# Three expert weight chunks loaded inside the last RWKV head pair, and token-row stores put behind four chunk loads

## The reference, cut to what matters

```python
for i in range(DEPTH):                       # DEPTH = 2
    h = rms_norm(x, norm_mix_g[i])
    mix = rwkv7_time_mix(h, ...) if i % 2 == 0 else mla_mix(h, ...)
    x = x + mix
    x = x + expert_choice_ffn(rms_norm(x, norm_ffn_g[i]), moe_router[i],
                              moe_w_gate[i], moe_w_up[i], moe_w_down[i])

def expert_choice_ffn(h, w_router, w_gate, w_up, w_down):
    aff = softmax(h @ w_router)                       # over 16 experts
    gates, idx = top_k(swapaxes(aff, 1, 2), 64)       # 64 tokens for each expert
    xe = h[b_idx, idx]
    hid = silu(xe @ w_gate) * (xe @ w_up)
    return zeros_like(h).at[b_idx, idx].add((hid @ w_down) * gates)
```

## Time and profile before

| what | value |
|---|---|
| timed runs, median (lowest to highest) | 1900.12 us (1898.45 to 1905.87) |
| profiled execution, own time | 1901.98 us |
| its span | 1900.2 us |
| TensorE busy in the span | 1772.0 us (93%) |
| VectorE, ScalarE, GpSimd busy | 819.0, 559.6, 153.1 us |
| bytes moved, mean | 459.69 MB, 242 GB/s |
| last RWKV pair, from its first to its last product | 529.6 to about 591.8 us |
| first product with an expert weight, layer 0 | 666.76 us |
| last product of layer 0's experts | about 1110 us |

### The profile page before, as it was taken

The page is one execution under the profiler, slowest core; times in us unless marked ns, Lnnn a source line. Parts: engine busy times, 40 slices in busy tenths (PEclk is TensorE's granted clock), DMA queues, the critical chain, the costliest instruction groups (busy, mean ns, idle before and its releaser), DMA issues.

```text
span 1900.2 us, 40296 instructions
## 1 busy us (share of the span) xinstructions
PE 1772.0 (93%) x17576; PEld 898.3 (47%) x17576; DVE 819.0 (43%) x1562; ACT 559.6 (29%) x1161; POOL 153.1 (8%) x230
## 2 busy tenths in 40 slices
PE   7999999999999599999988998999996999999998
PEld 4456666666555333333333355666543333333333
DVE  7867777776653412222211234777414222112212
ACT  3456555655542111111110123555320111101110
POOL 2101110111011100000000011111120000000000
PEclk9999999999999799999999998999997999999999
DMA  4101101110314999999999942000276999999998
GB/s 130 37 19 45 38 24 35 45 38 24 110 69 150 366 377 427 428 427 427 427 428 426 417 165 112 24 24 25 98 304 249 428 427 428 427 427 428 427 428 343
DMA packets 92184, 459.69 MB, mean 242 GB/s; under 512 B 16997, under 2 KB 50154, under 8 KB 68202
## 3 DMA queue, kind: packets, MB, share of 16 engines
q1 hardware_dynamic: 89994, 449.78, 58.5%
q0 software_dynamic: 2016, 7.34, 1.0%
HBM read 449.23 MB, written 7.86 MB: 241 GB/s over the span
## 4 chain that ended last, share of the span: by engine, by line
PE 73%; DMA 10%; issue 7%; DVE 3%; ACT 2%; SPq 2%; DVEq 1%; POOL 1%; POOLq 1%; another core or an unknown queue 1%; ACTq 0%; PEldq 0%
PE banks L1780 26%; PE banks L549 9%; DMA arena<-in_moe_w_down 7%; PE banks L1802 5%; PE banks L854 4%; PE banks L1433 4%; DMA arena<-in_moe_w_up 3%; PE banks L2355 3%; PE banks L2220 2%; PE banks L2380 1%; PE banks L2368 1%; PE banks L834 1%; PE banks L566 1%; SPq L1957 1%; PE banks L1748 1%
## 5 line engine op out<-in xcount | busy, mean ns | idle before, releaser
L1780 PE MATMUL banks<-arena 128*64 128x512 f32 x2944 | 657.4, 601 | 32.1 <-DMA arena<-in_moe_w_down 20.2
L1780 PEld LDWEIGHTS banks<-arena 128*64 128x64 f32 x2944 | 209.7, 138 | 442.7 <-issue 411.3
L1945 DVE TENSOR_TENSOR arena<-arena,banks 128x512 f32<-128x512 f32 x128 | 88.1, 688 | 285.1 <-PE banks L1802 285.1
L549 PE MATMUL banks<-arena 128*128 128x512 f32 x384 | 192.1, 618 | 0.0
L1885 ACT ACTIVATE arena<-banks 128x512 f32<-128x512 f32 x32 | 34.1, 1066 | 394.1 <-PE banks L1780 394.1
L1929 DVE SCALAR_TENSOR_TENSOR arena<-arena,banks 128x512 f32<-128x512 f32 x32 | 34.1, 1064 | 217.7 <-ACT arena L1885 217.7
L1802 PE MATMUL banks<-arena 128*128 128x512 f32 x256 | 114.7, 598 | 1.5 <-DVE arena L1942 1.5
L854 PEld LDWEIGHTS banks<-arena 64*64 64x64 f32 x5120 | 83.7, 134 | 62.9 <-issue 51.4
L1932 DVE SCALAR_TENSOR_TENSOR arena<-arena,small,banks 128x512 f32<-128x512 f32 x32 | 35.6, 1112 | 174.6 <-PE banks L1780 174.6
L854 PE MATMUL banks<-arena 64*64 64x64 f32 x5120 | 95.0, 221 | 2.6 <-issue 0.9
L549 PEld LDWEIGHTS banks<-arena 128*128 128x128 f32 x384 | 64.8, 189 | 51.5 <-issue 43.1
(11 more groups left out here) (307 smaller groups left out, 2217.7 us busy)
## 6 DMA issues: line engine op xcount, KB each, us to landing
arena<-in_moe_w_gate SPq DMA_DIRECT2D x64, 2048.0 KB, 32.5
arena<-in_moe_w_up SPq DMA_DIRECT2D x64, 2048.0 KB, 35.1
arena<-in_moe_w_down SPq DMA_DIRECT2D x54, 2048.0 KB, 36.2
arena<-in_moe_w_down SPq DMA_DIRECT2D x24, 512.0 KB, 11.6
arena<-in_moe_w_down SPq DMA_DIRECT2D x8, 1024.0 KB, 26.1
arena<-in_x SPq DMA_DIRECT2D x8, 512.0 KB, 7.5
arena<-in_rw_wr SPq DMA_DIRECT2D x8, 512.0 KB, 4.3
arena<-in_rw_wk SPq DMA_DIRECT2D x8, 512.0 KB, 4.2
```

What stands on the lines that cost most here:

```text
L549: last = nc.tensor.matmul(b[:, :], w_sl[:, n, k, :], xmix[n][:, k, :], start=(k == 0), stop=(k == ND - 1))
L1780: last = nc.tensor.matmul(b[z * CAP:(z + 1) * CAP, :], st[:, k, :], ring[g % RING][:, k, z * 512:(z + 1) * 512], start=(c % 2 == 0 and k = ...
L1945: nc.vector.tensor_tensor(xs, xs, b[:, :], ALU.add).then_inc(free[xj[("add", i, j)][0]], 1)
```

## The change

Placement. The tiles of the RWKV pairs are given new addresses. Eight prepared inputs (`rT, kT, kkn, kraw, cs, cx, e_neg, in_chunk`), `tw`, `ta`, the even parity of `AR` and `y_out` now fill the first three slots, `RING0` to `RING0 + 3 * CHUNK`. Tiles that the last pair, u = 7, still uses (`Bt`, `Kt`, the odd parity of `AR`, `rk_cols`, the block matrices) stay below `RING0`; `vT`, `ysq`, `bonus` go behind the third slot. No computing instruction is added, removed or reordered: the rows of TensorE, VectorE, ScalarE and GpSimd, with their waits, are the same in both kernels.

SP's program. In the last pair, before anything else of that pair, SP waits until the operands of pair 7 are complete, and then three times for a level of the inversion, `("U", 0, 1, 7)`, `("U", 2, 1, 7)` and `("U", 4, 1, 7)`, issuing chunk 0, 1 and 2 behind them. In layer 0 `load_experts` then starts with chunks 3, 8 and 10 alone, stores token tiles 0 and 1, loads 4, 5, 6 and 7, and stores tiles 2 and 3 behind chunk 7. Layer 1 keeps its order.

```diff
-        in_chunk = body(S)
         head_ones = body(P)
-
-        rT, kT, vT, kkn, kraw, cs, cx, rk_cols, e_neg = (body(S) for _ in range(9))
-        tw, ta = [body(S) for _ in range(2)], [body(S) for _ in range(2)]
+        rk_cols = body(S)
         Bt = [body(S) for _ in range(2)]
         Kt = [body(S) for _ in range(2)]
-        AR = [[body(2, NCH, CH) for _ in range(2)] for _ in range(2)]
+        AR_last = [body(2, NCH, CH) for _ in range(2)]
...
-        ysq = body(S)
+        PREPARED = 3
+        prepared = place(RING0)
+        in_chunk = prepared(S)
+        rT, kT, kkn, kraw, cs, cx, e_neg = (prepared(S) for _ in range(7))
+        tw, ta = [prepared(S) for _ in range(2)], [prepared(S) for _ in range(2)]
+        AR = [[prepared(2, NCH, CH) for _ in range(2)], AR_last]
+        y_out = [prepared(S) for _ in range(2)]
+        assert prepared.at[0] <= RING0 + PREPARED * CHUNK and NPAIR % 2 == 0
+
+        body = place(RING0 + PREPARED * CHUNK)
+        vT, ysq = body(S), body(S)
         bonus = [body(S) for _ in range(2)]
-        y_out = [body(S) for _ in range(2)]
...
-            for g in (0, 1, 2, 3, KEPT + 1, KEPT + 3) if layer == 0 else (0, 1, 2, 3, 4, KEPT + 1, KEPT + 3):
+            for g in (3, KEPT + 1, KEPT + 3) if layer == 0 else (0, 1, 2, 3, 4, KEPT + 1, KEPT + 3):
                 load_chunk(sp, layer, g)
...
-            for t in range(NT - 1):
+            for t in range(2 if layer == 0 else 3):
                 store_tokens(t)
             job_full(sp, ojs[layer], ("out", NT - 1, 1))
             for g in (4, 5, 6) if layer == 0 else (5, 6):
                 load_chunk(sp, layer, g)
             sp.wait_ge(hT_read[layer], 1)
             load_chunk(sp, layer, KEPT)
-            store_tokens(NT - 1)
+            for t in range(2 if layer == 0 else 3, NT):
+                store_tokens(t)
             sp.wait_ge(routed[layer], 1)
             load_chunk(sp, layer, KEPT + 2)
...
             for u in range(NPAIR):
+                if u == NPAIR - 1:
+                    sp.wait_ge(operands_ready, 2 * (NPAIR - 1))
+                    for g in range(PREPARED):
+                        job_full(sp, rj, ("U", 2 * g, 1, u))
+                        load_chunk(sp, 0, g)
                 if 0 < u < NPAIR - 1:
```

More of the change, by code:

```diff
@@ L157, in trunk @@
         eye = body(CH)
-        in_chunk = body(S)
         head_ones = body(P)
-        rT, kT, vT, kkn, kraw, cs, cx, rk_cols, e_neg = (body(S) for _ in range(9))
-        tw, ta = [body(S) for _ in range(2)], [body(S) for _ in range(2)]
+        rk_cols = body(S)
         Bt = [body(S) for _ in range(2)]
         Kt = [body(S) for _ in range(2)]
-        AR = [[body(2, NCH, CH) for _ in range(2)] for _ in range(2)]
+        AR_last = [body(2, NCH, CH) for _ in range(2)]
         blocks_at = body.at[0]
         body(ND * S)
+        assert body.at[0] <= RING0
         over = place(blocks_at)
```

## The result

The changed kernel took 1905.81 us (median of 20 runs, 1901.84 to 1908.62), the kernel before 1901.74 us (20 runs, 1897.84 to 1906.49). The ratio is 1.0020 with a 95% interval of 1.0012 to 1.0028, a loss of 2.3 to 5.3 us. It is measurable over 20 runs, but under the 0.5% at which one measurement of this kernel tells a change.

What follows compares the result with a forecast made beforehand. The prediction took layer 0 as bound by TensorE's start with the experts plus a fixed-length weight stream. Its terms, 0 + 0 + 0 + 3 + 0 = +3 us, gave 1903 us beside 1900.12, range 1895 to 1911.

Steps and rivals of the forecast that it cites:

- The bound: Layer 0's experts: the time TensorE begins with them, plus a weight stream of fixed length behind it.
- The rival by which the stream gains 14.7 us: Layer 0's experts: weights bound from the first chunk on, so 14.7 us leave the stage, 1885.4 us; chance 0.06.
- The early chunks' head start, 0: Layer 0's stream: loading chunks 0 to 2 in the last pair only lengthens DMA gaps; gain 0.
- The stores, 0: Stores of tiles 2 and 3, queued behind four chunks, stay hidden by 15 us of cover; cost 0.
- the addresses, 0: New tile addresses: no duration depends on the address; cost 0, bounds -1 to +1 us.
- Starved TensorE, +3: Last pair: early chunk loads delay TensorE's instruction fetch; cost 3 us, bounds 0 to 14 us.
- the step that I took from pair 6: Pair 6's idle beside the 4.2 MB projection load, which cost 5.2 us, taken as guide for the last pair's loads.
- What would show it: Changed profile's expected signs: issues near 545.4, 560.5, 571.4 us; idle of 0.5 to 2 us behind second and third chunks.
- my bound of 6: Last pair: the prediction is wrong if TensorE's "issue" idle grows by over 6 us.

Runs made afterwards that it cites:

- e9: Kernel before with chunks 8 and 10 loaded behind chunk 9, after the routing, instead of at 602 us; ratio 1.0027.
- e2: Changed kernel with only chunks 0 and 1 early, chunk 2 back at the head of the expert loads; ratio 1.0007 to the kernel before.
- e10: Kernel before with the projection load in four, new addresses, new store order and chunks 0 and 1 early; ratio 0.9999.
- e7: Kernel before with its 4 MB output projection load cut into four pieces spread through pair 6; 1897.69 us, ratio 0.9983.
- e1: Changed kernel without the early loads and with the old store order, so the new addresses alone; 1900.68 us, ratio 0.9994 to the kernel before.
- e5: Kernel before with the changed kernel's order of stores alone; ratio 1.0012.
- e11: Changed kernel with the old order of stores, all three chunks still early; ratio 1.0028 to the kernel before.
- e4: Changed kernel with 32 extra products in pair 0's bonus job, shifting TensorE's later code; ratio 1.0114 to the kernel before.
- e6: Changed kernel with chunk 2 alone early, chunks 0 and 1 back at the head of the expert loads; ratio 1.0020 to the kernel before.
- e3: Changed kernel with all three chunks issued in one burst behind the inversion's last level; ratio 1.0019 to the kernel before.

## Why the prediction was right

**The bound.** Right. Chunk 12 follows TensorE's use of chunk 1, 11.79 us behind the first expert product in all fourteen traces, however early the first eleven chunks came. The rival by which the stream gains 14.7 us failed at the point named, full slots and dry windows. What I did not size was how much slack that is; e9 puts it near 5.6 us.

**The early chunks' head start, 0.** Right: no gain in the changed kernel, in e2 against before or in e10 against e7.

**The stores, 0, and the addresses, 0.** e1 bears out the second within 0.14%. For the first e5 and e11 leave 0.2% either way.

**Starved TensorE, +3.** The mechanism was right, and the step that I took from pair 6; e4 and the times of the packets show it. That the size came out near is in part luck. I chose 3 out of bounds of 0 to 14, by bytes and with a discount for the late onset; the timed loss is 4.07 us between medians, and the stretch from L999, where chunk 2's cost lies, is 2.3 us longer in the profiled execution (3.8 in e6, 4.1 in e3 and e11). The split was less good. I gave 0.5, 1 and 1.5 us to chunks 0, 1 and 2; measured were 0, 0.26 and 1.99 us of idle, so chunk 2 was under-sized and the others over-sized. What makes the difference is where a block border falls, which I had no count for; e4, with 128 records of shift, gives 1.74 us to chunk 1 and 0.38 to chunk 2. I also left the clock behind the idle out of the 3 us. It was granted at 0.58 and 0.57 in e6 and e11, which cost 1.7 and 1.6 us beside the idle, and at 1.00 in the profiled execution of the changed kernel. That such spells lift the timed loss above 3 us is likely, not shown: how many of the timed executions had one isn't recorded. The idle of 0.80 us before L999 in pair 6, which I named beside the 3.04, need not be the projection's: it stands at 0.79 in e7 too, and at no block border.

**What would show it.** Issues at 544.9, 559.9 and 571.3 us, for 545.4, 560.5 and 571.4. Chunk 12 is 9.8 us behind the first refill half. Behind the third chunk came 1.99 us of idle, behind the second 0.26, less than the 0.5 that I had put at least. Behind the new first group the DMA share was 0.22 for 12 us, not near 0, since the stores run there. Waits for weights in layer 0 rose to 18.0 us where I said 16; e1 has 17.7 without a loss, so that is scatter. The sum of new idle is 2.25 us, inside my bound of 6.

## What to carry to other kernels

Before loading weights earlier, find the wait at which the stream really starts: where a ring's slots are all full and the DMA engines run dry ahead of it, an earlier load only lengthens that gap. And ask what the transfer will run beside: in a stretch of many small products even 2 MB can hold up the instruction fetch, so cut a large load into pieces with code between them, or put it where single instructions are long. Count instructions between idle "issue" rows; if the distances are multiples of one number, and the rows move when instructions are added ahead of them, the fetch is the first suspect.

## What the runs showed of the hardware

TensorE's instructions came in blocks of 256 records, about 251 of them products and weight loads, by packets of 16.4 KB. Five of its idle rows in the changed kernel stood exactly 2 or 4 such blocks apart. At a border with over 1 us of idle in pairs 6 and 7 TensorE went on 2.2 to 2.5 us after a packet began. At L1033 in pair 6 and at its counterpart in pair 7, a load's traffic put off the start of the packet by 2.4 to 3.7 us, and the packet itself took no longer, so the block was late by 2.0 to 3.3 us, in a 15 us burst as in a 5 us one. At other borders the same 2 MB cost 0.26 to 1.74 us. Code can be dense enough to idle without any load: the kernel before has 0.30 us before 559.49 with 0 to 8 GB/s of traffic around it. The Trainium skill (Runtime: NRT & Kernel Launch, section Instruction fetch mechanics) gives the same block of 256 instructions and calls its fetch mostly hidden; here 3.04 us of one border weren't, and cutting one load in four gave 3.9 us back.

Idle of 2.0 us cost 2.3 us in the stretch from L999 once, and idle of 2.2 to 2.5 us cost 3.8 to 4.1 at other times, where the clock was then granted at its lower level for part of the next 4 or 8 us. The same code at the same place did both; TensorE had been busy for 2.01 of the 4 us before in the one case, for 1.84 and 1.46 in e6 and e11.
